# Nine orders and owners in a streaming encoder layer: norms, weight split, attention scaling, zeros

## The chip, the cores and the metric

The kernel runs on one core of one Trainium2 chip. TensorE (PE) multiplies matrices, VectorE (DVE) and ScalarE (ACT) work on vectors, GpSimd (POOL) helps, and SyncE (SP) issues most DMAs. The metric is the device time of one execution in microseconds; less is better. Three runs of the kernel before gave 1050.23, 1053.16 and 1054.89 us.

## The reference

One layer of an encoder on 544 tokens: 512 of a new stream (four tiles of 128) and 32 of a running stream (the tile called SAMPLE, number 4). All weights are float32.

```
h   = RMSNorm(x);  c = h @ w_in                       # 1824 + 1536 + 2048 columns
A   = RWKV-7 time mixing of c: token shift, LoRA decay/rate/gate,
      per-token matrix state S (8 heads, 64x64), head layer norm, + bonus, * gate
Bd  = differential attention, 4 heads; RMSNorm over each head's 128 outputs
      * subln * (1 - lam_init)
mix = sigmoid(gA) * (A @ w_out_a) + sigmoid(gB) * (Bd @ w_out_b)
x   = x + RMSNorm(mix @ w_o)
x   = x + RMSNorm(SwiGLU(RMSNorm(x)))                 # D_FF = 2816
```

Besides the two outputs the layer gives new keys, values, the state S and the last shifted row of each stream.

## The kernel before

Every large product is made in three passes of a rounded format: a weight w is split into w_hi (rounded) and w_lo = w - w_hi, an activation likewise, and PE adds hi*hi, hi*lo and lo*hi into one accumulator (`three`). Channels lie on partitions, tokens on columns, 272 of them to a bank. A block of 128 output channels over all 544 tokens is one "dense" step, and two accumulators of two banks (dps) take turns. Four further banks (side) serve everything else in turn: each step of the list takes the next bank, and PE may write it only after the reader four fills earlier has drained it.

Weights come in units of 128 x 1024 (512 KB). SP loads unit u into one of two raw buffers once POOL has split unit u-2 (`w_split`); POOL splits it (L718 w_hi, L723 w_lo) into one of two slots once PE has finished the last block that uses the slot (`seg_done`). POOL starts unit after unit at the dense steps of its own queue, so its other work (the start of the block inverse, "xi"; the affine part of the group norm, "yrs", L787 to L798; the diagonal blocks, L782) stands between them.

One list, `schedule()`, gives the order of all steps, and each engine walks through it and issues its own part, so every engine has a fixed queue. The parts of the list that matter here:

- The first norm. normA squares a tile on ACT and scales it on DVE (L1638); normB transposes it on PE (L1055), ACT copies h_hi, DVE subtracts h_lo (L1607). The first two blocks of c are done in token halves: tiles 0 and 1 first, then tiles 2, 3 and 4. SP issues the loads of x, the constants (cst) and some twenty-five small parameters before unit 2's weight load.
- Attention. attS, attC, attP and attO are one head of one tile. After all heads of the prompt, "oscale" makes the reciprocals, "oA" scales a tile's heads by its reciprocal and by subln (DVE, L1699), "ofin" transposes it on PE and splits it into o_hi (ACT) and o_lo (DVE). Pieces of the gate projections (gB, gA) are woven in as filler for PE.
- The state stage, from about 280 to 555 us. For each tile a 128 x 128 triangular inverse is built in levels: wm (PE product, DVE mask L1821), wd (PE product, DVE subtraction L1829, then an expansion L1614 or L1834 with a transpose L1837), wt (PE transpose, ACT copy). Two groups g of four heads go side by side. Beside the inverse of tile t+1 run the chain of states of tile t (chain0, q, ya, yb, chain1, L928 to L963) and the group norm of tile t-1: ymean, yvar, yrs, then yfin (the gate's product on PE L1184, L1185, gating on DVE L1869) and ysplit (y_hi on ACT L1443, y_lo on DVE L1875, which releases the bank).
- "init0" zeroes three buffers on DVE (L1760 to L1762) and then lets ACT load the running stream's state into one of them (L1378).
- The output projections. outB needs o; outE does blocks 0 to 5 for tiles 0 and 1, outL and outA the rest once the last group norm is split. DVE multiplies by the gate and adds outB's part, ACT and DVE split the result into S (L1993 to L2011, L1522, L1525). Units of outE are split on POOL at the steps of outE.
- "zw" and "zS" gather the sums of squares of the later norms (L1895, L1913), make the root on ACT (L1474) and the reciprocal on DVE (L1916).

## Time and profile before

| | us |
|---|---|
| median of three runs | 1053.16 |
| the profiled execution | 1049.86 |
| its span | 1048.1 |
| PE busy | 995.7 |
| DVE busy | 463.5 |
| ACT busy | 277.5 |
| POOL busy | 552.8 |

In a timeline row the first number is the start in microseconds from the span's start, the second how long the row's instructions took together, then engine, line, instruction, output and inputs, and how many there were. In square brackets stands how long the engine was idle before, and which engine's instruction released it. "SPq" and "ACTq" are DMA issues in an engine's queue. In a row of the chain of waits there are start, length, engine and line. A row of the windows gives busy time and count for PE, PEld (weight load), DVE, ACT and POOL, then the granted clock of PE as a share of full speed, the DMA share and GB/s. Full speed is 2.4 GHz, and the other level is 1.2 GHz.

### The profile page before, as it was taken

How to read it: one execution, taken by the hardware profiler on the slowest of the kernel's cores; microseconds unless marked ns; L12 is line 12 of the kernel's file. 1: busy time of each engine (PE TensorE's matmuls, PEld its weight loads, DVE VectorE, ACT ScalarE, POOL GpSimd, SP SyncE). 2: the span in 40 equal slices, each digit the busy share in tenths (PEclk: the TensorE clock that was granted, in tenths of full speed). 3: DMA queues.
4: the chain of work that ended last, by engine and by line, in shares of the span. 5: the costliest groups of instructions: out<-in, count | busy, mean ns of one | idle time of the engine just before them, and what ended most of it. 6: DMA issues, size and time to landing. Idle time of an engine off the chain costs nothing.

```text
span 1048.1 us, 22126 instructions
## 1 busy us (share of the span) xinstructions
PE 995.7 (95%) x8886; PEld 942.4 (90%) x8886; DVE 463.5 (44%) x895; ACT 277.5 (26%) x788; POOL 552.8 (53%) x605
## 2 busy tenths in 40 slices
PE   5899999999999999989988998999999999999996
PEld 4899999988878887878888998999999999999996
DVE  4456478277666455555445354333333333200003
ACT  4223354245533123322211353100110100011101
POOL 4677899633444134241446812565565565656571
PEclk9999999999999999999999999999999999999999
DMA  8232322432223100132014612322322323232332
GB/s 267 62 82 81 81 70 72 124 113 72 66 73 83 38 32 33 33 119 106 26 54 133 184 45 61 98 82 80 100 80 83 97 80 90 83 93 76 93 91 86
DMA packets 138111, 89.70 MB, mean 86 GB/s; under 512 B 5258, under 2 KB 130032, under 8 KB 138032
## 3 DMA queue, kind: packets, MB, share of 16 engines
q1 hardware_dynamic: 129508, 73.17, 24.4%
q10 hardware_dynamic: 8524, 15.42, 4.2%
q8 instruction: 56, 0.92, 0.4%
q14 instruction: 23, 0.19, 0.1%
HBM read 79.39 MB, written 9.19 MB: 85 GB/s over the span
## 4 chain that ended last, share of the span: by engine, by line
PE 83%; DVE 8%; POOL 3%; ACT 2%; issue 2%; DMA 1%; ACTq 0%; DVEq 0%; SPq 0%; POOLq 0%
PE dense L981 67%; PE side L1055 3%; PE side L1098 1%; POOL w_lo L723 1%; PE side L933 1%; PE side L1124 1%; DVE gt L1793 1%; PE side L907 1%; PE side L897 1%; PE side L1175 1%; DMA xs<-in_x_prompt 1%; PE side L963 1%; PE side L847 1%; PE side L928 1%; DVE z L1937 1%
## 5 line engine op out<-in xcount | busy, mean ns | idle before, releaser
L718 POOL TENSOR_SCALAR w_hi<-w_raw 128x256 fp32r<-128x256 f32 (+1 forms) x256 | 158.4, 637 | 369.7 <-PE dense L981 360.0
L723 POOL TENSOR_TENSOR w_lo<-w_raw,w_hi 128x256 fp32r<-128x256 f32 (+1 forms) x256 | 321.4, 1277 | 9.8
L981 PE MATMUL dense<-h_hi,w_hi 128*128 128x272 f32 (+2 forms) x1392 | 303.6, 296 | 10.4 <-DVE h_lo L1607 6.9
L981 PE MATMUL dense<-h_hi,w_lo 128*128 128x272 f32 (+2 forms) x1392 | 295.0, 290 | 0.0
L981 PE MATMUL dense<-h_lo,w_hi 128*128 128x272 f32 (+2 forms) x1392 | 294.2, 289 | 0.0
L981 PEld LDWEIGHTS dense<-h_hi,w_hi 128*128 128x128 f32 x1392 | 221.7, 190 | 21.3 <-issue 8.6
L981 PEld LDWEIGHTS dense<-h_lo,w_hi 128*128 128x128 f32 x1392 | 222.4, 190 | 0.0
L981 PEld LDWEIGHTS dense<-h_hi,w_lo 128*128 128x128 f32 x1392 | 221.4, 190 | 0.0
L981 PE MATMUL dense<-S,w_hi 128*128 128x272 f32 (+2 forms) x648 | 109.2, 289 | 0.0
L981 PEld LDWEIGHTS dense<-S,w_hi 128*128 128x128 f32 x648 | 92.2, 188 | 0.1
L981 PE MATMUL dense<-S,w_lo 128*128 128x272 f32 (+2 forms) x324 | 68.2, 288 | 0.0
L1971 DVE SCALAR_TENSOR_TENSOR S<-z,S 128x544 f32 (+1 forms) x22 | 53.5, 2430 | 22.5 <-ACT S L1502 22.5
L1965 DVE TENSOR_TENSOR z<-z,dense 128x544 f32<-128x544 f32 (+2 forms) x23 | 15.9, 696 | 97.1 <-PE dense L981 97.1
L1904 DVE TENSOR_TENSOR z<-side,gain 128x512 f32<-128x512 f32 x7 | 4.8, 691 | 114.6 <-ACT h_hi L1465 114.6
L981 PEld LDWEIGHTS dense<-S,w_lo 128*128 128x128 f32 x324 | 51.1, 188 | 0.0
L1502 ACT ACTIVATE S<-z 128x544 f32 (+1 forms) x22 | 14.5, 661 | 132.3 <-DVE z L1965 132.3
L981 PE MATMUL dense<-S 128*128 128x288 f32 (+1 forms) x336 | 45.3, 291 | 0.0
L981 PEld LDWEIGHTS dense<-S 128*128 128x128 f32 x336 | 42.8, 188 | 0.4 <-DVE S L2011 0.2
L1960 DVE SCALAR_TENSOR_TENSOR z<-z,dense 128x544 f32<-128x544 f32 (+2 forms) x23 | 15.9, 696 | 59.2 <-ACT z L1495 55.3
L1495 ACT ACTIVATE z<-dense 128x544 f32<-128x544 f32 x21 | 13.1, 625 | 97.4 <-PE dense L981 97.4
L792 POOL TENSOR_TENSOR AR<-AR 128x256 f32<-128x256 f32 (+1 forms) x10 | 6.5, 650 | 52.7 <-DVE AR L1860 52.7
L1291 ACT ACTIVATE early<-side,amax 128x128 f32<-128x128 f32 (+4 forms) x40 | 19.9, 499 | 35.7 <-DVE amax L1673 35.6
(270 smaller groups left out, 1393.3 us busy)
## 6 DMA issues: line engine op xcount, KB each, us to landing
w_raw<-in_w_ffn_in SPq DMA_DIRECT2D x44, 512.0 KB, 3.8
w_raw<-in_w_in SPq DMA_DIRECT2D x43, 512.0 KB, 3.9
w_raw<-in_w_ffn_out SPq DMA_DIRECT2D x16, 448.0 KB, 3.6
gates<-gst ACTq DMA_DIRECT2D x16, 272.0 KB, 2.0
w_raw<-in_w_o SPq DMA_DIRECT2D x8, 512.0 KB, 3.8
w_raw<-in_w_ffn_out SPq DMA_DIRECT2D x8, 512.0 KB, 3.7
w_raw<-in_w_out_a SPq DMA_DIRECT2D x5, 512.0 KB, 3.5
mb<-gates ACTq DMA_DIRECT2D x1, 2176.0 KB, 8.7
```

Of the source, the lines that this page charges most:

```text
L718: ins = nc.gpsimd.tensor_scalar(hi[:, q], w_raw[:, slot, q], 1.0, 0.0, ALU.mult, ALU.add)
L723: ins = nc.gpsimd.tensor_tensor(lo[:, q], w_raw[:, slot, q], hi[:, q].bitcast(F32), ALU.subtract)
L847: ins = pe.matmul(b[32 * q:32 * q + 32, 0:64], xt[:, g, q, :], mce[:, g, q, :], start=True, stop=True)
L897: ins = pe.matmul(b[0:n, h * 64:(h + 1) * 64], gt[0:n, g, h, 0:n], tok[0:n, g, 2, h, :], start=True, stop=True)
L981: ins = pe.matmul(acc[:, bk, 0:tn], w, r[:, t0:t0 + tn], start=first and n == 0, stop=final and n == 2)
L1055: ins = pe.transpose(b[0:m, c0:c0 + n], src, ident[0:n, 0:n])
L1291: drain(f_act(probs[0:n, pb, m, 0:keys], b[0:n, 0:keys], ACT.Exp, bias=amax[0:n, 2 * pb + m:2 * pb + m + 1], scale=SCALE, accum_out=asum[0 ...
L1495: f_act(f_t.rearrange("p (a b) -> p a b", a=2), pa[:, :, 0:HALF], ACT.Tanh, scale=0.5).then_inc(s_["f_tanh"], 1)
L1502: f_act(dst, f_s.unsqueeze(1), ACT.Copy, scale=0.5).then_inc(s_["f_hi"], 1)
L1960: ins = vec.scalar_tensor_tensor(out=fs, in0=ft, scalar=1.0, in1=ga_, op0=ALU.add, op1=ALU.mult)
L1965: ins = vec.tensor_tensor(fs, fs, gb_, ALU.mult)
L1971: vec.scalar_tensor_tensor(out=lo, in0=f_s.unsqueeze(1), scalar=0.5, in1=hi.bitcast(F32), op0=ALU.mult, op1=ALU.subtract).then_inc(s_["f_l ...
```

## The change

Nine edits, none of which changes what is computed:

1. The norm of tiles 2 and 3 moves ahead: the third tile is transposed before the first dense group, the fourth before the second.
2. Unit 0 gets split buffers of its own (w0_hi, w0_lo), and unit 2's split has no wait on PE. On SP the small parameters are issued after unit 2's load, the constants before it.
3. oA moves from DVE to ACT, scaling by the reciprocal alone. subln is loaded as one value per partition and applied in ofin, behind the transpose, by ACT and DVE.
4. The three memsets move from DVE to POOL, which waits for the last ofin; ACT's load of the state moves behind the next three steps (init1); DVE waits for the zeros at its first "e".
5. In wd, DVE subtracts for both groups first and expands both afterwards.
6. yfin and ysplit of a tile are issued one tile later, after "e" and a filler, and in the order g0, g0, g1, g1.
7. POOL splits the second outE unit at the second half of outB 7, and the third at outE 1.
8. outA's mixing is done in two halves of 272 tokens.
9. The sums of squares are reduced in zw, before the product, no longer in zS.

```diff
@@ -104,6 +104,7 @@
 OUT_LATE = [("outL", 2), ("outL", 3), ("outL", 4), ("outL", 5), ("outA", 6), ("outA", 7), ("outL", 0), ("outL", 1)]
+MIX_PIECE = {d: sum(1 + (e[0] == "outA") for e in OUT_LATE[:n]) for n, d in enumerate(OUT_LATE)}
@@ -184,7 +185,7 @@
     rows = [[(st, t, g) for g in range(2)] for st in ("ymean", "yvar", "yrs")[:2 + (t >= SAMPLE - 1)]]
-    return rows + [[(st, t, g) for st in ("yfin", "ysplit") for g in range(2)]]
+    return rows + [[(st, t, g) for g in range(2) for st in ("yfin", "ysplit")]]
@@ -212,7 +213,7 @@
     norms = skew(NT, "normA", "normB")
-    s = norms[:5] + first_pair[:1] + norms[5:7] + first_pair[1:2] + norms[7:] + first_pair[2:] + [("params",)]
+    s = norms[:7] + first_pair[:1] + norms[7:9] + first_pair[1:2] + norms[9:] + first_pair[2:] + [("params",)]
@@ -276,17 +277,18 @@
         s += [("ofin", t)] + filler(t < SAMPLE)
-    s += weave([[("init0",)]] + first[-3:], [filler(1) for _ in range(3)])
+    s += weave([[("init0",)]] + first[-3:], [filler(1) for _ in range(3)]) + [("init1",)]
+    yfin = []
...
-        s += filler(t == SAMPLE) + both("wu", t) + filler(t == SAMPLE) + both("e", t) + filler(1)
+        s += filler(t == SAMPLE) + both("wu", t) + filler(t == SAMPLE) + both("e", t) + filler(1) + yfin
...
-                s += weave(invert_rows(t + 1), [c00, ymean, f0, c01, yvar, f1, q, [], f2, ya, f3, yfin, c10, f4, c11])
+                s += weave(invert_rows(t + 1), [c00, ymean, f0, c01, yvar, f1, q, [], f2, ya, f3, [], c10, f4, c11])
@@ -441,6 +443,9 @@
     ga = sb("ga", [P, 8, TOK], at=phase2)
+    w0_hi = sb("w0_hi", [P, D], F32R, at=region)
+    w0_lo = sb("w0_lo", [P, D], F32R, at=region)
+    region.close()
@@ -488,7 +493,7 @@
     orst = sb("orst", [P, NT * BH], at=phase2)
-    subln = sb("subln", [P, BV], at=phase2)
+    subln = sb("subln", [P, 1], at=phase2)
@@ -580,6 +585,15 @@
+
+    def mix_halves(d):
...
+        i, acc = d[1], dps[BLOCK[d] % 2]
+        if d[0] == "outA":
+            cuts = [(bk * HALF, HALF, acc[:, bk, 0:HALF]) for bk in range(2)]
+        else:
+            cuts = [(2 * P, TOK - 2 * P, acc[:, 0, 0:TOK - 2 * P])]
+        return [(S[:, i, 0, a:a + n], S[:, i, 1, a:a + n], ga[:, i, a:a + n], mb[:, i, a:a + n], c) for a, n, c in cuts]
@@ -643,7 +657,6 @@
         def load_parameters():
-            sp.dma_start(cst[:, :], i_["cst"][:, :]).then_inc(s_["cst_loaded"], 16)
@@ -659,7 +672,7 @@
                 sp.dma_start(lamv[:, n, :], i_[name][0].partition_broadcast(P)).then_inc(s_["att_loaded"], 16)
-            sp.dma_start(subln[:, :], i_["diff_subln"][0].partition_broadcast(P)).then_inc(s_["att_loaded"], 16)
+            sp.dma_start(subln[:, :], i_["diff_subln"][0].rearrange("(p o) -> p o", o=1)).then_inc(s_["att_loaded"], 16)
@@ -673,6 +686,8 @@
                 x_load(SAMPLE)
+                sp.dma_start(cst[:, :], i_["cst"][:, :]).then_inc(s_["cst_loaded"], 16)
+            elif u == 3:
@@ -735,10 +750,10 @@
             else:
-                hi, lo = w_hi[:, u % 2, :], w_lo[:, u % 2, :]
-                if u >= 2:
...
-                    v = next(v for v in range(u - 2, -1, -2) if UNITS[v][0] != "woA" or UNITS[v][1] == 5)
+                hi, lo = (w_hi[:, u % 2, :], w_lo[:, u % 2, :]) if u else (w0_hi[:, :], w0_lo[:, :])
+                if u >= 3:
...
+                    v = next(v for v in range(u - 2, 0, -2) if UNITS[v][0] != "woA" or UNITS[v][1] == 5)
@@ -760,7 +775,9 @@
                 ahead = UNIT_OF[step[1:3]][-1][0] + 1
-                units_up_to(min(ahead, UNIT_OF[("outE", OUT_EARLY[-1])][0][0]) if step[1] == "outE" else ahead)
+                units_up_to(min(ahead + step[2] % 2, UNIT_OF[("outE", OUT_EARLY[-1])][0][0]) if step[1] == "outE" else ahead)
+            elif step == ("dense", "outB", 7, 1, 2):
+                units_up_to(UNIT_OF[("outE", 2)][0][0])
@@ -776,6 +793,13 @@
                                         ALU.add).then_inc(s_["xb_init"], 1)
+            elif k == "init0":
...
+                pool.wait_ge(s_["rw_done"], CT)
+                landed(pool, ("ofin", SAMPLE), "o")
+                G(nc.gpsimd.memset(sio[:, :, :], 0.0))
+                G(nc.gpsimd.memset(ebd[:, :, :, :, :], 0.0))
+                nc.gpsimd.memset(mbd[:, :, :, :, :], 0.0).then_inc(s_["zeroed"], 1)
@@ -1028,6 +1052,8 @@
                     hi, lo = w_hi[:, u % 2, c:c + P], w_lo[:, u % 2, c:c + P]
+                    if u == 0:
+                        hi, lo = w0_hi[:, c:c + P], w0_lo[:, c:c + P]
@@ -1314,8 +1340,19 @@
                 A.mark(f_act(orms[0:n, a:b_], ossq[0:n, a:b_], ACT.Sqrt, scale=1.0 / BV, bias=EPS), s_["o_rms"], "o_rms")
+            elif k == "oA":
+                t = step[1]
+                n = TILES[t][1]
+                act.wait_ge(s_["o_rst"], 1 + (t == SAMPLE))
+                for h in range(BH):
+                    o = otok[0:n, t, h * BV:(h + 1) * BV]
+                    ins = f_act(o, o, ACT.Copy, scale=orst[0:n, t * BH + h:t * BH + h + 1])
+                ins.then_inc(s_["o_scaled"], 1)
...
-                halves(o_hi, step, "o", *TILES[step[1]], "o_hi_done", 0)
+                t0, n = TILES[step[1]]
+                b = full_bank(act, step, "o")
+                f_act(o_hi[:, :, t0:t0 + n], b[:, 0:4 * n].rearrange("p (k n) -> p k n", k=4), ACT.Copy,
+                      scale=subln[:, :]).then_inc(s_["o_hi_done"], 1)
@@ -1371,7 +1408,7 @@
                 A.mark(f_act(t2, t2, ACT.Exp, scale=-1.0), s_["rw_e2"], "rw_e2")
-            elif k == "init0":
+            elif k == "init1":
@@ -1517,13 +1554,9 @@
                     turn = OUT_LATE.index(d)
-                    act.wait_ge(s_["mixed"], turn + 1)
-                    if kind == "outA":
-                        f_act(S[:, i, 0, :].rearrange("p (a b) -> p a b", a=2), dps[BLOCK[d] % 2][:, :, 0:HALF], ACT.Copy,
-                              scale=0.5).then_inc(s_["mix_hi"], 1)
-                    else:
-                        f_act(S[:, i, 0, 2 * P:TOK], dps[BLOCK[d] % 2][:, 0, 0:TOK - 2 * P], ACT.Copy, scale=0.5).then_inc(
-                            s_["mix_hi"], 1)
+                    for half, (hi, _, _, _, acc) in enumerate(mix_halves(d)):
+                        act.wait_ge(s_["mixed"], MIX_PIECE[d] + half + 1)
+                        f_act(hi, acc, ACT.Copy, scale=0.5).then_inc(s_["mix_hi"], 1)
@@ -1690,19 +1723,15 @@
                 dve.wait_ge(s_["o_rms"], step[1] + 1)
-                V(vec.reciprocal(orst[0:n, a:b_], orms[0:n, a:b_]))
-            elif k == "oA":
-                t = step[1]
-                n = TILES[t][1]
-                for h in range(BH):
-                    o = otok[0:n, t, h * BV:(h + 1) * BV]
-                    ins = vec.scalar_tensor_tensor(out=o, in0=o, scalar=orst[0:n, t * BH + h:t * BH + h + 1],
-                                                   in1=subln[0:n, :], op0=ALU.mult, op1=ALU.mult)
-                V.mark(ins, s_["o_scaled"], "o_scaled")
+                V.mark(vec.reciprocal(orst[0:n, a:b_], orms[0:n, a:b_]), s_["o_rst"], "o_rst")
...
-                low(o_hi, o_lo, step, "o", t0, n, "o_hi_done", t + 1, 0)
+                b = full_bank(dve, step, "o")
+                dve.wait_ge(s_["o_hi_done"], t + 1)
+                drain(vec.scalar_tensor_tensor(out=o_lo[:, :, t0:t0 + n], in0=b[:, 0:4 * n].rearrange("p (k n) -> p k n", k=4),
+                                               scalar=subln[:, :], in1=o_hi[:, :, t0:t0 + n].bitcast(F32), op0=ALU.mult,
+                                               op1=ALU.subtract), step, "o")
@@ -1755,11 +1784,6 @@
                 V.mark(vec.tensor_tensor(kx, kx, t2, ALU.mult), s_["rw_done"], "rw_done")
-            elif k == "init0":
...
-                V(vec.memset(sio[:, :, :], 0.0))
-                V(vec.memset(ebd[:, :, :, :], 0.0))
-                V.mark(vec.memset(mbd[:, :, :, :, :], 0.0), s_["zeroed"], "zeroed")
@@ -1793,6 +1817,8 @@
                 elif st == "e":
+                    if (t, g) == (0, 0):
+                        dve.wait_ge(s_["zeroed"], 1)
@@ -1827,17 +1853,20 @@
                 drain(vec.tensor_tensor(xv, xv, b[0:n, 0:64].rearrange("p (b s) -> p b s", s=s), ALU.subtract), step, "d")
-                landed(dve, step, "d")
-                if lv + 1 < len(LEVELS):
-                    expand(lv + 1, t, g)
-                elif nblocks(t) > 1:
-                    V.mark(vec.tensor_tensor(xe32[:, g, :, :], xp[:, g, :].unsqueeze(1).broadcast_to([P, 2, P]),
-                                             cst[:, K_BB:K_BB + 4:2].unsqueeze(2).broadcast_to([P, 2, P]), ALU.mult),
-                           s_["xe_set"], "xe_set")
-                    V.mark(vec.transpose(xb[:, g, :], xp[:, g, :]), s_["xb_last"], "xb_last")
-                else:
-                    V.mark(vec.transpose(xt64[0:n, g, :, 0:n], xp[0:n, g, :].rearrange("p (h i) -> p h i", h=4)),
-                           s_["x64_set"], "x64_set")
+                if g == 0:
+                    continue
+                for gg in range(2):
+                    landed(dve, (k, lv, t, gg), "d")
+                    if lv + 1 < len(LEVELS):
+                        expand(lv + 1, t, gg)
+                    elif nblocks(t) > 1:
+                        V.mark(vec.tensor_tensor(xe32[:, gg, :, :], xp[:, gg, :].unsqueeze(1).broadcast_to([P, 2, P]),
+                                                 cst[:, K_BB:K_BB + 4:2].unsqueeze(2).broadcast_to([P, 2, P]), ALU.mult),
+                               s_["xe_set"], "xe_set")
+                        V.mark(vec.transpose(xb[:, gg, :], xp[:, gg, :]), s_["xb_last"], "xb_last")
+                    else:
+                        V.mark(vec.transpose(xt64[0:n, gg, :, 0:n], xp[0:n, gg, :].rearrange("p (h i) -> p h i", h=4)),
+                               s_["x64_set"], "x64_set")
@@ -1887,6 +1916,9 @@
                 dve.wait_ge(s_["z_sq"], (i + 8 * (part == "B") if i < 8 else 30 + (part == "B")) + 1)
+                if i >= 7:
+                    for n, a, b_ in Z_SUMS[(i - 7, part)][1]:
+                        V.mark(vec.tensor_reduce(ssq[0:n, a:b_], zsq[0:n, a:b_, :], AX.X, ALU.add), s_["z_sum"], "z_sum")
@@ -1909,8 +1941,6 @@
                 first_sum, pieces = Z_SUMS[step[1:]]
-                for n, a, b_ in pieces:
-                    V.mark(vec.tensor_reduce(ssq[0:n, a:b_], zsq[0:n, a:b_, :], AX.X, ALU.add), s_["z_sum"], "z_sum")
@@ -1996,20 +2026,17 @@
+                    block_full(dve, d)
+                    halves = mix_halves(d)
...
+                    for _, _, gate, other, a2 in halves:
+                        V(vec.scalar_tensor_tensor(out=a2, in0=gate, scalar=1.0, in1=a2, op0=ALU.add, op1=ALU.mult))
+                        V.mark(vec.tensor_tensor(a2, a2, other, ALU.add), s_["mixed"], "mixed")
+                    for half, (hi, lo, _, _, a2) in enumerate(halves):
+                        dve.wait_ge(s_["mix_hi"], MIX_PIECE[d] + half + 1)
+                        ins = vec.scalar_tensor_tensor(out=lo, in0=a2, scalar=0.5, in1=hi.bitcast(F32), op0=ALU.mult,
+                                                       op1=ALU.subtract)
+                    ins.then_inc(block_sem(d), 1)
```

## Rows read from the trace of the kernel before

**Rows 1.** The page's busy times by engine, whole span.

```profile
PE 995.7 (95%) x8886; PEld 942.4 (90%) x8886; DVE 463.5 (44%) x895; ACT 277.5 (26%) x788; POOL 552.8 (53%) x605
```

**Rows 2.** Timeline, 0 to 45 us: start, length, engine, instruction, idle before.

```profile
11.02 1.97 PE L1055 MATMUL side<-ident,xn 128*128 128x128 f32 x8 [0.95 <-DVE xn L1638]
...
12.65 2.73 DVE L1638 SCALAR_TENSOR_TENSOR xn<-xs,rstd,gain 128x1024 f32<-128x1024 f32 x1
...
16.76 0.58 PE L981 MATMUL dense<-h_hi,w_hi 128*128 128x256 f32 x1 [3.77 <-DVE h_lo L1607]
...
18.84 23.77 SPq L693 DMA_DIRECT2D w_raw<-in_w_in  x4
...
28.49 0.40 PE L981 MATMUL dense<-h_hi,w_hi 128*128 128x288 f32 x1 [1.52 <-DVE h_lo L1607]
...
32.12 1.51 POOL L718 TENSOR_SCALAR w_hi<-w_raw 128x256 fp32r<-128x256 f32 x4 [11.51 <-PE dense L981]
...
36.65 0.49 PE L981 MATMUL dense<-h_hi,w_hi 128*128 128x272 f32 x2 [1.43 <-POOL w_lo L723]
```

**Rows 3.** Timeline, 279 to 298 us, end of attention.

```profile
279.50 0.28 ACT L1311 ACTIVATE otok<-side 128x128 f32<-128x128 f32 x1
...
288.90 1.82 DVE L1699 SCALAR_TENSOR_TENSOR otok<-otok,orst,subln 128x128 f32<-128x128 f32 x3
...
292.17 1.13 DVE L1699 SCALAR_TENSOR_TENSOR otok<-otok,orst,subln 128x128 f32<-128x128 f32 x4
...
297.07 0.30 PE L1055 MATMUL side<-ident,xp 128*128 128x128 f32 x1 [1.31 <-ACT early L1291]
```

**Rows 4.** Timeline: POOL's first memset, and 324 to 332 us.

```profile
0.75 0.52 POOL L757 MEMSET g2b<- 96x512 f32 x1 [0.29 <-POOLq L2031]
...
324.26 0.91 DVE L1761 MEMSET ebd<- 128x1024 f32 x1 [0.28 <-DVE C L1760]
...
326.39 1.36 ACTq L1378 DMA_DIRECT2D C<-in_state_wkv  x2
...
328.17 0.63 PE L850 MATMUL side<-xte,tc 128*32 128x128 f32 x8 [1.64 <-ACT tc L1406]
...
331.56 0.46 POOL L775 TENSOR_TENSOR xb<-wa,cst 128x128 f32<-128x128 f32 x1 [6.70 <-DVE wa L1775]
```

**Rows 5.** Timeline of PE, 366 us.

```profile
366.69 0.33 PE L1055 MATMUL side<-ident,xp 128*128 128x128 f32 x1 [0.73 <-DVE xp L1829]
```

**Rows 6.** Timeline of PE: the three waits for the split's bank.

```profile
414.06 0.34 PE L928 MATMUL side<-wu,tok 64*64 64x64 f32 x4 [1.39 <-DVE y_lo L1875]
...
459.76 0.34 PE L928 MATMUL side<-wu,tok 64*64 64x64 f32 x4 [2.00 <-DVE y_lo L1875]
...
504.18 0.34 PE L928 MATMUL side<-wu,tok 64*64 64x64 f32 x4 [0.84 <-DVE y_lo L1875]
```

**Rows 7.** Timeline, 534 to 575 us, output projections.

```profile
534.01 0.72 DVE L1986 SCALAR_TENSOR_TENSOR mb<-mb,dense 128x544 f32<-128x544 f32 x1 [1.15 <-PE dense L981]
...
542.54 0.83 PE L1055 MATMUL side<-ident,mbd 128*128 128x128 f32 x4 [0.74 <-ACT AR L1397]
...
545.00 0.36 PE L981 MATMUL dense<-y_hi,w_hi 128*128 128x256 f32 x1 [1.64 <-POOL w_lo L723]
...
555.69 0.37 PE L981 MATMUL dense<-y_hi,w_hi 128*128 128x288 f32 x1 [2.15 <-DVE y_lo L1875]
...
574.12 0.40 PE L981 MATMUL dense<-y_hi,w_hi 128*128 128x288 f32 x1 [1.16 <-DVE S L2011]
```

**Rows 8.** A row of the windows, and two of the chain: start, length.

```profile
556.00:560.00 4.00, 4.00 (x22) 4.00 (x21) 1.39 (x3) 0.41 (x1) 0.00 (x0) 0.61 0.00 0
...
285.83 1.49 PE dense L981 x12
...
461.51 3.02 PE dense L981 x12
```

**Rows 9.** Timeline of DVE at the end.

```profile
1041.73 0.16 DVE L1913 TENSOR_REDUCE ssq<-zsq 128x2 f32<-128x16 f32 x1
```

15 lines of the change are left out of this document (1 added, 14 removed).

## The prediction, made before the changed kernel was built

> **What bounds the kernel now.** I read the busy times first, then every TensorE (PE) wait in order of time, then the other engines around each wait. PE is busy 995.7 of 1048.1 us [rows 1], so 52.4 us are all that orders and owners can win, apart from PE's own pace. No PE instruction is added or removed by the change. The waits fall into places that the nine edits name: the first norm [rows 2], the end of attention [rows 3], the first state tile [rows 4], the block inverse [rows 5], the group norm's split [rows 6], the output projections [rows 7], the sums of squares [rows 9]. A second loss is pace: four stretches run at half clock, 1.2 instead of 2.4 GHz, three behind waits of 1.31, 2.00 and 2.15 us and one behind two short ones at 365.6 and 366.7. One window shows a granted mean of 0.61, and twelve dense matmuls take 3.02 us instead of 1.49 [rows 8].
>
> **The change part by part.** The sum is made against the profiled execution: span 1048.1, its own time 1049.86.
>
> *Norm order at the start.* PE stands 3.77 us before its first dense group, which waits for h_lo of tile 1; the normalised tile 2 is ready at 12.65+2.73=15.38 [rows 2]. Its eight transposes go in front of that group. At the half clock eight take 1.97, so they end at about 17.4, 0.6 after the old start of 16.76. Against this, about 0.9 leaves the full-clock part, some 0.5 comes back because less dense work falls before the clock rises, 0.2 because tiles 3 and 4 are transposed apart, and the 1.52 wait at 28.49 shrinks to about 0.6, since only the 32 rows of tile 4 are left to copy and subtract. +0.6-0.9-0.5-0.2-0.9 = -1.9. Bounds: -3.4 (both waits half gone and the 0.9) and 0.
>
> *Unit 0 in its own buffer, parameters behind unit 2's load.* Unit 2 is split only after PE has left unit 0 (POOL idle 11.51 until 32.12), and PE waits 1.43 for it at 36.65 [rows 2]. Now POOL goes on from unit 1 at about 20.7 and has unit 2 by 27, so the 1.43 goes. On SP's queue, unit 2's load leaves at about 14.4 instead of 18.84; some twenty-five parameter DMAs, 9.9 us of issue, come behind it, so unit 3's load leaves at about 24.4, while POOL wants it at 32. The parameter transposes on PE come at about 33, after the last of these has left at 24.3. -1.4; bounds -1.43 and 0. What speaks against it: POOL now works beside VectorE's (DVE's) norm of tile 4, and a norm beside a split took 2.73 [rows 2]; it would end at 23 and is wanted at 25, so this is hidden, by 2 us.
> The Trainium skill (SBUF — State Buffer, Who interferes with whom) says that DVE with two SBUF inputs and GpSimd lock each other out of one port pair, and that ScalarE never waits there. The trace agrees: the scaling took about 0.6 a piece beside a split and 0.28 without one [rows 3]. By that rule the scaling is worth up to its upper bound below, 1.31, and the sum of the waits would be 11.6 and not 10.75; the same rule speaks against the early split of unit 2.
>
> *Attention scaling on ScalarE (ACT).* Twenty DVE operations become twenty ACT copies of 0.28 [rows 3]: 1.1 us a tile. The pieces of tiles 0 and 1 stand before the masks and subtractions that lead to the wait of 1.31 at 297.07, but a dense group between them hides the first; 0.5 reaches PE. For tile 4 ACT must wait for a reciprocal that stands behind inverse work on DVE, and three copies of the transposed output queue behind it by about 3 us; PE has dense groups there and their banks come free in time: nothing. -0.5; bounds -1.31 and +1.1 (one tile's copies uncovered).
>
> *Zeros on POOL.* Three memsets on DVE (0.91 for 1024 columns) and 1.36 of DMA issue on ACT stand before the copy tc; PE waits 1.64 for it [rows 4]. POOL has 6.70 us idle up to 331.56; its own memset of 512 columns took 0.52, so 512+1024+1024 cost about 2.6, and it waits for the end of attention, which is over by then. The 1.64 goes. The two issues now stand before the token copies of tile 0: of 1.36 I let 0.5 reach PE through the banks. -1.1; bounds -1.64 and -0.3.
>
> *Both groups' subtractions before the expansions.* The second transpose waited 0.73 because the first group's expansion and DVE transpose stood before its subtraction [rows 5]: -0.7. In twenty such places the first group's expansion comes one subtraction (0.2) later. At the next steps a dense group of 1.5 covers that; uncovered it is +4.4.
>
> *Split a tile later, group by group.* PE waits 1.39, 2.00 and 0.84 for a bank that y_lo releases [rows 6], as gating stands behind the inverse's last level on DVE. At the new place, after e and a dense group, DVE has less before it, but each group is now a serial chain DVE, ACT, DVE of about 1.3, and the next chain0 reuses the bank: I take 0.35 there, and 0.25 where the removed matmuls covered the subtraction, twice, and 0.1 for the third tile. -4.23+1.3 = -2.9; bounds -4.2 and 0.
>
> *Early weight split.* The second outE unit is split behind the group norm's POOL work; PE waits 1.64 for it at 545.00 [rows 7]. It will be split from the end of outB 7 on, shortly before 534.01 [rows 7], in front of that work, which then starts 0.9 later and so frees the second bank of the final transposes later: that takes 1.5 of the 1.64 and of a wait of 0.74 before it [rows 7]. -0.9; bounds -2.4 and +1. *Group order at outL:* the first six matmuls need group 0 alone, ready 1.3 earlier, the next six group 1 as before: of 2.15 [rows 7] 0.65 goes; bounds -2.15 and 0. *Halved mixing:* of 1.16 [rows 7] 0.2, as six short DVE operations replace three; bounds -1.16 and +0.3. *Sums first:* a reduction of 0.16 [rows 9] and the square root pass the product, 0.25 on two chains, one of them the tail: -0.5; bounds -0.8 and 0.
>
> Sum of the waits: 1.9+1.4+0.5+1.1+0.7+2.9+0.9+0.65+0.2+0.5 = 10.75.
>
> *Clock.* Each half-clock stretch costs about 1.5 (3.02-1.49) [rows 8], four 6.0. Waits of 1.64 [rows 4, 7] are not followed by one, so idle time alone doesn't decide; I take half: -3.0, bounds -6 and +3 (two new ones).
> The Trainium skill (TensorE: Matmul & The Clock Gate, Part 1) says that the throttled state is the default and activity releases it. By that rule all four could go, which is the third rival.
>
> 10.75+3.0 = 13.75: the profiled 1049.86 becomes 1036.1. That execution lies 3.3 below the median of the runs shown (1053.16), so for a median I forecast 1053.16-13.75 = 1039.4, say **1040**, with a range of its own of 1034 to 1047.
>
> **Rivals.**
> *Slower: DVE's queue is the bound of the state stage.* Place: from 300 to 555 us. The late expansions cost 4.4 and five tiles' split pairs hold DVE for 2x1.3 each, 13, all seen by PE. The other terms (10.75 without 0.7 and 2.9) give back 7.15, with no clock gain: +10.3, 1063. For it: most PE waits there name DVE. Against: the three waits in [rows 6] sum to 4.23 in 90 us, and dense groups stand between the steps. It decides once more than about 1.2 of each 1.3 hold is uncovered.
> *The waits change place.* The bank wait after the split, the token copies and the late POOL work fill what was freed; only head, zeros and sums stay: 1.9+1.4+1.1+0.5 = 4.9, 1048. For it: each freed wait has a next one within 0.5 us in my reckoning.
> *The clock stays up.* 10.75+6.0: 1036. For it: each drop follows a wait that an edit names.
> *The change doesn't do what it says:* the new buffer and the order at SP bring unit 2 no earlier, as its load shares the DMA engines with the constants; then 1.4 less, 1041.5, inside the forecast.
>
> **How the numbers follow.** Forecast 0.60 (with the last rival), clock stays up 0.16, waits change place 0.17, slower 0.07. A measurement of this kernel tells 0.5%, 5.3 us, from no change. Faster: 0.60+0.16 and half of 0.17, 0.84; same 0.10, slower 0.06. The range of 8 in 10 is 1033 to 1049.
>
> **What would show it.** Right: the first dense matmul at about 17.4 behind three tiles' transposes, no POOL wait at 33; no wait at the copy tc; L928 without y_lo waits over 0.5; DVE without otok; POOL's outE unit before its AR work; fewer windows with a clock under 1. Wrong: PE's first wait behind yfin's transposes over 1 us; POOL's AR work so late that the final transposes wait over 2 us; the token copies holding sk by 1.3; as many half-clock stretches as before, elsewhere. If PE's idle time falls by less than 6 us the sum is wrong whatever the time says.

## The result, and the profile after

The kernel after took 1039.07 us in the median (1037.57 to 1040.89, four runs) against 1053.54 (1050.23 to 1054.89, four runs): ratio 0.9868, 95% interval 0.984 to 0.9896. Run again later in six runs it gave 1040.21 (1037.25 to 1041.94), ratio 0.9881 [0.9856, 0.9907] against eleven runs of before at 1052.05. The forecast was 1040. Its profiled execution took 1040.89 (span 1039.1), 1.8 above its median, while that of before lay 3.7 below its own; so the two traces differ by 9.0 us and the medians by 14.5.

The page's busy times after [rows 1]:

```profile
PE 993.6 (96%) x8886; PEld 939.6 (90%) x8886; DVE 451.2 (43%) x878; ACT 284.0 (27%) x810; POOL 557.1 (54%) x608
```

PE's idle time (span less busy) fell from 52.4 to 45.5, by 6.9 where the forecast had 10.75. PE's timeline after, at the places of [rows 2 to 7]:

```profile
15.45 1.97 PE L1081 MATMUL side<-ident,xn 128*128 128x128 f32 x8 [2.45 <-DVE xn L1671]
17.07 0.56 PE L1005 MATMUL dense<-h_hi,w_hi 128*128 128x256 f32 x1
...
26.64 0.40 PE L1005 MATMUL dense<-h_hi,w_hi 128*128 128x288 f32 x1 [0.76 <-DVE h_lo L1640]
...
292.99 0.30 PE L1081 MATMUL side<-ident,xp 128*128 128x128 f32 x1 [0.41 <-ACT early L1317]
...
327.26 1.17 PE L911 MATMUL side<-AR,C 64*128 64x256 f32 x4 [0.42 <-ACT tok L1421]
...
425.74 0.34 PE L952 MATMUL side<-wu,tok 64*64 64x64 f32 x4 [0.43 <-DVE y_lo L1904]
...
470.63 0.34 PE L952 MATMUL side<-wu,tok 64*64 64x64 f32 x4 [0.41 <-DVE y_lo L1904]
...
533.12 0.41 PE L1081 MATMUL side<-ident,mbd 128*128 128x128 f32 x2 [2.03 <-DVE y_lo L1904]
538.09 0.73 PE L1201 MATMUL side<-AR,cst 128*128 128x64 f32 x4 [1.26 <-ACT AR L1467]
544.36 0.37 PE L1005 MATMUL dense<-y_hi,w_hi 128*128 128x288 f32 x1 [0.93 <-DVE y_lo L1904]
545.85 0.58 PE L1005 MATMUL dense<-y_hi,w_hi 128*128 128x288 f32 x1 [0.45 <-DVE y_lo L1904]
...
563.27 0.40 PE L1005 MATMUL dense<-y_hi,w_hi 128*128 128x288 f32 x1 [1.18 <-DVE S L2037]
```

The waits of the head, of the first state tile and of the inverse are gone or small. Two of 2.03 and 1.26 at 533 and 538 are new, and so is one of 1.25 at 499.69, which the section on the experiments shows. Summed over the rows of its timeline, PE's waits went from 43.9 to 36.9 us: from 15.8 to 12.3 up to 100 us, from 14.6 to 9.6 between 290 and 520, from 6.5 up to 8.3 between 520 and 600, and from 4.5 to 4.2 behind.

The clock: before, four stretches lay under full speed [rows 8]; after, one. PE's windows of 4 us after (the clock is the third number from the end):

```profile
544.00:548.00 4.00, 3.19 (x15) 3.02 (x16) 0.95 (x4) 0.23 (x1) 0.76 (x3) 0.73 0.00 0
548.00:552.00 4.00, 3.60 (x23) 3.37 (x21) 2.43 (x7) 0.82 (x2) 1.75 (x2) 0.84 0.00 0
```

Every run lists its mean granted clock. Eleven runs of before average 0.9915, six of after 0.9965. Over 1050 us that is some 9.0 and 3.6 us lost to the clock, 5.4 less. With 7.0 of waits it makes 12.4, an estimate that lies between the two measured differences of the medians, 14.5 and 11.8. It mixes the waits of one execution with the clock of many. Within the profiled pair the mean clocks are 0.992 and 0.996, about 4 us apart; with 7.0 that makes 11, and 9.0 were measured, since some 2 us came back inside PE's busy time.

### The profile page after: what moved, and what is told of

It reads as the page before. It is cut to its first block, busy times and chain, and to the rows that moved or that the text cites. A ratio compares the mean times of both kernels' runs of the same rounds, so it can differ in the third digit from the quotient of the medians.

```text
span 1039.1 us, 22129 instructions
## 1 busy us (share of the span) xinstructions
PE 993.6 (96%) x8886; PEld 939.6 (90%) x8886; DVE 451.2 (43%) x878; ACT 284.0 (27%) x810; POOL 557.1 (54%) x608
## 4 chain that ended last, share of the span: by engine, by line
PE 82%; DVE 6%; POOL 4%; DMA 3%; ACT 3%; issue 1%; ACTq 0%; DVEq 0%; SPq 0%; POOLq 0%
PE dense L1005 66%; PE side L1081 3%; DMA w_raw<-in_w_o 2%; POOL w_lo L738 1%; PE side L1124 1%; PE side L1150 1%; PE side L957 1%; POOL S L738 1%; PE side L931 1%; PE side L921 1%; PE side L1201 1%; DMA xs<-in_x_prompt 1%; PE side L911 1%; PE side L871 1%; PE side L987 1%
## 5 line engine op out<-in xcount | busy, mean ns | idle before, releaser
L1005 PE MATMUL dense<-h_hi,w_hi 128*128 128x272 f32 (+2 forms) x1392 | 302.7, 295 | 4.4 <-DVE h_lo L1640 2.5
L1005 PE MATMUL dense<-h_hi,w_lo 128*128 128x272 f32 (+2 forms) x1392 | 293.8, 289 | 0.0
L1005 PE MATMUL dense<-h_lo,w_hi 128*128 128x272 f32 (+2 forms) x1392 | 293.1, 288 | 0.0
L1005 PEld LDWEIGHTS dense<-h_hi,w_hi 128*128 128x128 f32 x1392 | 220.9, 189 | 15.0 <-issue 7.0
L1005 PEld LDWEIGHTS dense<-h_lo,w_hi 128*128 128x128 f32 x1392 | 221.4, 189 | 0.0
L1005 PEld LDWEIGHTS dense<-h_hi,w_lo 128*128 128x128 f32 x1392 | 220.2, 189 | 0.0
L1005 PE MATMUL dense<-S,w_hi 128*128 128x272 f32 (+2 forms) x648 | 109.2, 289 | 0.1
L1005 PEld LDWEIGHTS dense<-S,w_hi 128*128 128x128 f32 x648 | 92.2, 188 | 0.5 <-issue 0.4
L1005 PE MATMUL dense<-S,w_lo 128*128 128x272 f32 (+2 forms) x324 | 68.2, 288 | 0.0
L1005 PEld LDWEIGHTS dense<-S,w_lo 128*128 128x128 f32 x324 | 51.1, 188 | 0.0
L1539 ACT ACTIVATE S<-z 128x544 f32 (+1 forms) x22 | 14.5, 659 | 132.3 <-DVE z L1995 132.3
L1005 PE MATMUL dense<-S 128*128 128x288 f32 (+1 forms) x336 | 45.3, 291 | 1.7 <-POOL S L738 1.7
L1005 PEld LDWEIGHTS dense<-S 128*128 128x128 f32 x336 | 42.8, 188 | 2.5 <-issue 2.2
```

Of the source, the lines that this page charges most:

```text
L1005: ins = pe.matmul(acc[:, bk, 0:tn], w, r[:, t0:t0 + tn], start=first and n == 0, stop=final and n == 2)
L1539: f_act(dst, f_s.unsqueeze(1), ACT.Copy, scale=0.5).then_inc(s_["f_hi"], 1)
```

## The experiments

Each of the first eight undoes one part of the change in the kernel after. They ran once each, beside single runs of before at 1053.80 and 1054.77. The profiled spans of the kernel after itself were 1039.1 and 1036.4 in two executions, so an end time under 3 us apart says nothing here, and I read them by the wait at its place and by the distance between two marks with the same work between them. Three marks serve: the wait for the first weight split at about 104 (L1005 w_lo), the waits for `gain` that begin the inverse of each tile (308.94, 350.22, 392.82 and 437.92 after), and the last wait for S at 563.27.

### The norm's order

```diff
-    s = norms[:7] + first_pair[:1] + norms[7:9] + first_pair[1:2] + norms[9:] + first_pair[2:] + [("params",)]
+    s = norms[:5] + first_pair[:1] + norms[5:7] + first_pair[1:2] + norms[7:] + first_pair[2:] + [("params",)]
```

> The changed kernel with edit 1 undone (norm steps in the old order). The waits-add-up theory: the group of tiles 2 to 4 of the first block starts at about 28.5 instead of 26.64, with a wait near 1.5 in front of it, and every later mark up to 540 us lies 1.8 later; span about 1041. The theory that waits change place: the 1.8 is there at 30 us but less than 0.5 of it at 540.

1044.14, span 1042.4. The mark at 104.49 came at 108.49, 4.0 later. The waits up to there grew from 12.3 to 14.25, and the next two windows hold a half-clock stretch that neither before nor after has; PE's wait and the windows of this kernel:

```profile
29.12 0.41 PE L1005 MATMUL dense<-h_hi,w_hi 128*128 128x288 f32 x1 [1.52 <-DVE h_lo L1640]
```

```profile
28.00:32.00 4.00, 2.88 (x13) 2.88 (x14) 1.07 (x4) 0.08 (x1) 0.00 (x0) 0.67 0.86 228
32.00:36.00 4.00, 4.00 (x29) 4.00 (x29) 0.00 (x0) 0.75 (x3) 0.00 (x0) 0.90 0.17 47
```

Without that stretch (about 1.5) the order is worth about 2.5, against a forecast of 1.9, and it isn't given back: the four `gain` marks, too, lie 3.9 to 4.0 later. The same wait of 1.52 was followed by no stretch before [rows 2].

### Unit 0's buffer and the parameters' place

```diff
-                hi, lo = (w_hi[:, u % 2, :], w_lo[:, u % 2, :]) if u else (w0_hi[:, :], w0_lo[:, :])
-                if u >= 3:
+                hi, lo = w_hi[:, u % 2, :], w_lo[:, u % 2, :]
+                if u >= 2:
...
-            elif u == 3:
+            elif u == 2:
                 load_parameters()
```

> Edit 2 undone alone (unit 0 in slot 0, parameters issued before unit 2's load). Waits add up: PE waits about 1.4 for w_lo at about 34.8, and later marks up to 540 us lie 1.4 later; span about 1040.5. Waits change place: the POOL wait of 0.96 at 104.5 shrinks by as much, and nothing is left at 200 us.

1040.99, span 1039.2. The wait is back, whole, but the mark at 104 is only 0.6 later than after's, where 1.4 was forecast (in the eleven traces with this part and the norm's new order it stood at 103.62 to 104.94, so it is 0.2 to 1.5 later than there). The wait for POOL behind that mark is 0.96 as before, so the 1.45 was not given back there:

```profile
34.07 0.49 PE L1004 MATMUL dense<-h_hi,w_hi 128*128 128x272 f32 x2 [1.45 <-POOL w_lo L737]
```

### The attention's scaling back on VectorE, subln left behind the transpose

```diff
-                act.wait_ge(s_["o_rst"], 1 + (t == SAMPLE))
...
-                    ins = f_act(o, o, ACT.Copy, scale=orst[0:n, t * BH + h:t * BH + h + 1])
+                    ins = vec.tensor_scalar(o, o, orst[0:n, t * BH + h:t * BH + h + 1], None, ALU.mult)
```

> The scaling of attention's output by the reciprocal goes back from ACT to DVE (as a multiplication by one value per partition; subln stays in ofin). Prediction's step: the wait of 0.41 at 293.0 becomes 0.9 to 1.3, later marks lie 0.5 to 0.9 later, and perhaps a half-clock stretch comes back behind it (1.5 more). Rival, ACT's own queue was the cost of the move: marks at 310 us lie earlier than in the changed kernel, as tile 4's scaling no longer holds ACT.

1035.23, span 1033.4, the shortest of all. DVE's scaling and PE's wait in this kernel, then ACT's scaling in the kernel after:

```profile
285.34 2.37 DVE L1724 TENSOR_SCALAR otok<-otok,orst 128x128 f32<-128x128 f32 x4
...
288.42 0.86 DVE L1724 TENSOR_SCALAR otok<-otok,orst 128x128 f32<-128x128 f32 x4
...
292.64 1.79 DVE L1724 TENSOR_SCALAR otok<-otok,orst 128x128 f32<-128x128 f32 x8
...
292.81 0.30 PE L1081 MATMUL side<-ident,xp 128*128 128x128 f32 x1 [0.62 <-ACT early L1317]
```

```profile
293.27 1.27 ACT L1349 ACTIVATE otok<-otok,orst 128x128 f32<-128x128 f32 x4
...
295.31 1.26 ACT L1349 ACTIVATE otok<-otok,orst 128x128 f32<-128x128 f32 x4
```

The wait is 0.2 longer on DVE, but from it to the first `gain` mark this kernel takes 15.16 and every one of the twelve other traces of this study 15.94 to 15.97, since ACT's copies stand in front of the inverse's copies there: the new owner costs 0.6. The eight operations in front of the wait take 3.23 here (2.37 + 0.86) and took 3.69 before (four from 288.90 on in 2.56, of which [rows 3] shows three, and four in 1.13), so dropping subln saves DVE under 0.5 us there. The wait is 0.7 shorter than before's 1.31 with DVE as owner in both kernels. The rest of the way to after's end (1039.1, and 1036.4 in its second trace) is not the owner: there is no half-clock stretch in this trace and no wait for weights at 580 to 592, places that the edit doesn't touch.
The Trainium skill (SBUF — State Buffer, Who interferes with whom) has DVE and GpSimd lock each other out of a shared port pair.
The trace agrees, for the form without subln too: POOL split from 285.52 to 288.32, and the four operations at 285.34 took 0.59 each, while those at 288.42 and 292.64, where POOL stood idle, took 0.22.

### Zeros back on VectorE

```diff
-                G(nc.gpsimd.memset(ebd[:, :, :, :, :], 0.0))
-                nc.gpsimd.memset(mbd[:, :, :, :, :], 0.0).then_inc(s_["zeroed"], 1)
+                V(vec.memset(ebd[:, :, :, :], 0.0))
+                V.mark(vec.memset(mbd[:, :, :, :, :], 0.0), s_["zeroed"], "zeroed")
```

> Edit 4 undone: memsets on DVE, the load of the state before the next three steps. Waits add up: the 1.64 in front of the last inverse product comes back, the 0.42 before sk goes and sk's products take 2.45 instead of 3.00, so marks at 337 lie 1.1 later (0.7 to 1.6). If the two DMA issues had cost PE nothing in the new place, 1.6 later.

1041.98, span 1040.2. From the first to the second `gain` mark 43.20, after 41.28: the part is worth 1.9, over the bound of 1.64. PE's wait of this kernel, and POOL's memsets of the kernel after:

```profile
323.01 0.63 PE L867 MATMUL side<-xte,tc 128*32 128x128 f32 x8 [2.04 <-ACT tc L1436]
```

```profile
320.09 0.52 POOL L800 MEMSET C<- 128x512 f32 x1
320.67 0.95 POOL L801 MEMSET ebd<- 128x1024 f32 x1
321.68 0.95 POOL L802 MEMSET mbd<- 128x1024 f32 x1
```

A memset costs nearly the same on both engines (0.91 on DVE in [rows 4]), and POOL still waited 2.47 us for its next work at 325.10. The two DMA issues held the token copies for 0.42 (at 327.26 above), near the 0.5 forecast; this kernel has no such wait, and its products there take 2.45 where those of after take 3.00. But it waits 0.90 for rb at 334.30, as before did at 339.47. So 2.04 + 0.90 go and 0.42 + 0.55 come, 1.97 in all, close to the 1.9 measured.

### One group's subtraction and expansion at a time

```diff
-                if g == 0:
-                    continue
-                for gg in range(2):
-                    landed(dve, (k, lv, t, gg), "d")
...
+                landed(dve, step, "d")
+                if lv + 1 < len(LEVELS):
+                    expand(lv + 1, t, g)
```

> Edit 5 undone: each group's subtraction and expansion together. Prediction's step: a wait of about 0.7 before the second transpose of the last level in each of the tiles 1 to 3 (at 360, 402 and 448 us), so 2.2 later at 460, and perhaps a half-clock stretch again. The slower rival (late expansions cost 0.2 in each of twenty places): marks at 460 lie up to 4 earlier than in the changed kernel, or the 0.7s are paid for by as much elsewhere.

1042.80, span 1041.0. PE's waits of this kernel:

```profile
361.37 0.33 PE L1081 MATMUL side<-ident,xp 128*128 128x128 f32 x1 [0.73 <-DVE xp L1855]
...
406.21 0.33 PE L1081 MATMUL side<-ident,xp 128*128 128x128 f32 x1 [0.83 <-DVE xp L1855]
...
451.68 0.33 PE L1081 MATMUL side<-ident,xp 128*128 128x128 f32 x1 [0.73 <-DVE xp L1855]
```

One wait [rows 5] was in the trace of before; three come back. For the other two tiles the trace of before shows what covered them: not another wait, but work. Sixteen products of yfin (L1184, L1185) stood between the inverse's product and the second transpose, which then waited for nothing; the bank wait of 1.39 [rows 6] comes behind it.

```profile
410.03 0.43 PE L847 MATMUL side<-gain,xt 128*32 128x64 f32 x16
410.39 0.49 PE L1184 MATMUL side<-C,g2a 128*128 128x128 f32 x2
...
412.06 0.39 PE L1185 MATMUL side<-C,g2b 128*128 128x128 f32 x2
412.28 0.38 PE L1055 MATMUL side<-ident,xp 128*128 128x128 f32 x2
```

Edit 6 takes these products away from there, and so makes two of the three waits that edit 5 removes. The stretch from 350.22 to 461.47 takes 3.5 longer, 1.4 of it a half-clock stretch at 360 to 368, so about 2.1 without the clock. That is what was expected of this run (2.2), and three times the 0.7 of the prediction, which had the old place in view.

### The split's old place, and its old order too

```diff
-        s += ... both("e", t) + filler(1) + yfin
-                s += weave(invert_rows(t + 1), [c00, ymean, f0, c01, yvar, f1, q, [], f2, ya, f3, [], c10, f4, c11])
+        s += ... both("e", t) + filler(1)
+                s += weave(invert_rows(t + 1), [c00, ymean, f0, c01, yvar, f1, q, [], f2, ya, f3, yfin, c10, f4, c11])
```

That is the first kernel, with the new order of groups; the second has the old order as well:

```diff
-    return rows + [[(st, t, g) for g in range(2) for st in ("yfin", "ysplit")]]
+    return rows + [[(st, t, g) for st in ("yfin", "ysplit") for g in range(2)]]
```

> Only the place of edit 6 undone; the order g0, g0, g1, g1 stays. If the place is what counts, as I think: waits for y_lo as in the old place with the old order, 1.4, 2.0 and 0.8 at L952, since gating stands behind the inverse on DVE; the two waits at outL stay 0.93 and 0.45. If the order is what counts, the waits at L952 stay under 0.6.

> Edit 6 undone whole: old place and old order of the group norm's split. Waits add up: L952 (the chain's first product) waits 1.4, 2.0 and 0.8 for y_lo at about 405, 450 and 492 and no longer 0.43 and 0.41, so the mark of outE 0 lies 2.9 to 3.4 later, 4.5 if a half-clock stretch follows one of them; the wait at outL is 2.1 in one piece and not 0.93 and 0.45. DVE's-queue rival: less than 1 later.

1038.08 (span 1036.3) and 1042.69 (span 1040.5). With the old place the bank waits are back, with 1.20, 1.06 and 0.43; the first two of that kernel:

```profile
404.29 0.34 PE L952 MATMUL side<-wu,tok 64*64 64x64 f32 x4 [1.20 <-DVE y_lo L1904]
...
449.23 0.34 PE L952 MATMUL side<-wu,tok 64*64 64x64 f32 x4 [1.06 <-DVE y_lo L1904]
```

And yet the place gains nothing in these executions: from the third `gain` mark to the last wait for S, PE waits 11.8 after, 10.6 with the old place and 10.8 with place and order undone. The stretch itself takes 170.45, 167.36 and 170.34, of which half-clock stretches cost 1.7, 0 and 5.1 by the granted clock. At the bank the new place wins 1.85 (2.69 less 0.43 + 0.41), and more than that is lost at 499.69 and 538.09, 1.25 + 1.26. ACT writes each final state into one small buffer and stores it by a DMA, and the second group's copy waits until the first one's store has landed. ACT's rows, of the kernel after and of the old place:

```profile
495.54 0.39 ACTq L1247 DMA_DIRECT2D out_wkv_prompt<-dtmp  x1
499.06 0.27 ACT L1458 ACTIVATE dtmp<-side 64x128 f32<-64x128 f32 x1 [3.56 <-DMA out_wkv_prompt<-dtmp]
...
536.74 0.27 ACT L1458 ACTIVATE dtmp<-side 64x128 f32<-64x128 f32 x1 [3.62 <-DMA out_wkv_sample<-dtmp]
```

```profile
497.59 0.38 ACTq L1247 DMA_DIRECT2D out_wkv_prompt<-dtmp  x1
499.33 0.27 ACT L1458 ACTIVATE dtmp<-side 64x128 f32<-64x128 f32 x1 [1.77 <-DMA out_wkv_prompt<-dtmp]
```

In before, too, it landed in 1.77. The obvious suspect for the doubling, the next weight load, is ruled out. SP issues it at 497.99 after and at 500.04 with the old place, 2.45 behind the first store in both, and 2.43 to 2.46 behind it in all fourteen traces, late or not. Its packets come later still: in the window from 498.50 to 499.00, the last before ACT goes on, the DMA engines move nothing (share and GB/s are the last two numbers).

```profile
498.50:499.00 0.50, 0.00 (x0) 0.00 (x0) 0.00 (x0) 0.00 (x0) 0.00 (x0) 1.00 0.00 0
499.00:499.50 0.50, 0.00 (x0) 0.00 (x0) 0.00 (x0) 0.41 (x2) 0.00 (x0) 1.00 0.41 84
```

What was under way besides the store is in the DMA queues of the window from 495.54 to 498.50 after (packets, MB, share), and of 497.59 to 500.50 with the old place:

```profile
q10 hardware_dynamic: 272, 0.07, 11.4%
q8 instruction: 1, 0.02, 3.1%
```

```profile
q10 hardware_dynamic: 272, 0.07, 10.7%
```

The 272 packets are the store. The other is one packet of 16 KB in the queue named "instruction"; it took 1.48 us from 496.32 on, and the store's last seventeen packets, some 4 KB, began only at 497.79. Of the twelve traces in which ACT waits for these stores, 24 stores in all, fifteen landed after 2.3 to 3.8 us, and each of them had such a packet in flight before its own last one; nine landed in 1.76 to 1.78, and none of them had. So the lateness goes with where an instruction packet falls, which edit 6 doesn't set by itself: the kernel with edit 5 undone has the new place and both stores in time. No run changes that packet alone, so this cause is read from the traces and not tested.

The spread that it leaves is wide: the kernels with the norm's order or unit 0 undone differ from after only in the first 40 us, and PE waits 10.2 in this stretch in both. With two store buffers and the new place (below) it waits 9.2, 1.4 less than with the old place. In each of these three the clock costs 3.4 here, and a slower PE waits less, so the numbers flatter the new place.

The group order alone does its work: with it undone the wait at outL is 2.14, after 0.93 + 0.45, 0.76 less (forecast 0.65).

### The weight split in its old place

```diff
-                units_up_to(min(ahead + step[2] % 2, UNIT_OF[("outE", OUT_EARLY[-1])][0][0]) if step[1] == "outE" else ahead)
-            elif step == ("dense", "outB", 7, 1, 2):
-                units_up_to(UNIT_OF[("outE", 2)][0][0])
+                units_up_to(min(ahead, UNIT_OF[("outE", OUT_EARLY[-1])][0][0]) if step[1] == "outE" else ahead)
```

> Edit 7 undone: outE's later units split at outE's own steps. Prediction's step: the wait of 2.03 before the second final transpose shrinks to about 1.2, a wait of 1.6 for w_lo comes back before outE 2, the mark of outL lies 0.4 to 0.9 later. Rival, the early split gained nothing because it delays the group norm on POOL by as much: outL's mark within 0.3.

1037.90, span 1036.1. PE's two waits of this kernel, then POOL's work in the kernel after:

```profile
531.18 0.41 PE L1079 MATMUL side<-ident,mbd 128*128 128x128 f32 x2 [0.97 <-DVE y_lo L1902]
...
533.21 0.36 PE L1003 MATMUL dense<-y_hi,w_hi 128*128 128x256 f32 x1 [1.62 <-POOL w_lo L738]
```

```profile
523.15 1.05 POOL L733 TENSOR_SCALAR w_hi<-w_raw 128x1024 fp32r<-128x1024 f32 x1 [11.49 <-PE dense L1005]
524.29 2.37 POOL L738 TENSOR_TENSOR w_lo<-w_raw,w_hi 128x1024 fp32r<-128x1024 f32 x1
526.62 0.73 POOL L816 TENSOR_TENSOR AR<-AR 128x256 f32<-128x256 f32 x1
```

0.97 + 1.62 = 2.59 undone; 2.03 + 1.26 = 3.29 after, of which the 1.26 is the store again. The w_lo wait of 1.62 goes, as forecast, but the group norm's POOL work starts at 526.62 instead of 524.67, 1.95 later where I had 0.9, and the final transposes wait 1.06 longer for it; the store takes the rest. Counted from the fourth `gain` mark, outL's first wait comes 1.4 earlier with edit 7 undone (542.72 after 437.69, against 544.36 after 437.92), which neither expectation allowed; 1.26 + 0.66 of longer store waits make up all of it (here the first store wait is 0.59, the second absent). Without the stores the edit gains 0.56; as it ran, it was worth nothing, against -0.9.

### Versions that go on from there

> The changed kernel again, beside the three variants on the same chip. Its ratio to the kernel before lies within 0.985 to 0.989; spans near 1039, one half-clock stretch near 548 us, and PE waits of about 0.4 and 1.3 for POOL's w_o units near 579 and 592.

This is the kernel after once more, five rounds; the three that follow ran beside it on the same chip.

```diff
-            sout = dtmp[:, 0:2 * 64].rearrange("p (k v) -> p k v", k=2)
+            sout2 = [dtmp[:, a:a + 2 * 64].rearrange("p (k v) -> p k v", k=2) for a in (0, 2 * 64)]
...
+                sout = sout2[g]
+                if g == 0:
                     act.wait_ge(stored, 16 * n_stored[0])
```

> The changed kernel, with the final states stored from two buffers, so that ACT need not wait for the first store before it copies the second. The waits of 1.25 at 499.7 and 1.26 at 538.1 go, so outL's mark lies 2.5 earlier. Waits add up: the end too, span 1036.6. Given back at woA (POOL and the w_o loads set the pace there): the waits for POOL near 579 and 592 grow from 1.7 to about 3, and the end moves by less than 1.2.

1039.44 (1036.80 to 1039.58, five runs), ratio 0.9862 [0.9835, 0.9889]. With a buffer for each group's store ACT goes on at once, and both PE waits of 1.2 are gone:

```profile
495.42 0.39 ACTq L1247 DMA_DIRECT2D out_wkv_prompt<-dtmp  x1
495.86 0.27 ACT L1460 ACTIVATE dtmp<-side 64x128 f32<-64x128 f32 x1 [0.46 <-PE side L1081]
```

From the fourth `gain` mark to the last wait for S the waits sum to 6.98, after 9.55 and 9.83 in its two traces, and that stretch takes 123.55 instead of 125.35 and 125.28. So it is shown that the new waits came from the one buffer. The time follows less far: this trace has two half-clock stretches between 532 and 546, outL's first wait comes 1.6 earlier and not 2.5, and the median moves by 0.8, within the scatter.

The second loads of x elsewhere (tile 4 at woA 3, tiles 0 and 1 in woB):

```diff
-                    elif kind == "woA" and i in (2, 4, 6):
-                        x1_load({2: 4, 4: 0, 6: 1}[i])
+                    elif d == ("woA", 3):
+                        x1_load(4)
+                    elif kind == "woB" and i in (0, 2):
+                        x1_load(i // 2, "x1_early")
```

> The changed kernel, with x loaded again for tiles 0 and 1 during woB instead of woA, tile 4 at woA 3. Theory that the second loads of x delay w_o's loads on the same DMA engines: POOL's waits for w_o fall from 5.5 to about 3, PE's waits of 0.39 and 1.29 go, the end comes 1.5 to 2.5 earlier. Rival, POOL's own 3.45 per unit is the pace: its waits fall little, and the end moves under 0.5.

1039.48 (1037.67 to 1040.73), ratio 0.9875 [0.9848, 0.9902]. It was to free the DMA engines for the weights that PE waits for at woA in the kernel after:

```profile
575.86 1.05 POOL L733 TENSOR_SCALAR S<-w_raw 128x1024 fp32r<-128x1024 f32 x1 [2.27 <-DMA w_raw<-in_w_o]
```

```profile
591.99 0.78 PE L1005 MATMUL dense<-S 128*128 128x288 f32 x4 [1.29 <-POOL S L738]
```

The wait is not in its trace, but neither is it in the second trace of the kernel after, where POOL waited 0.93 at the same unit. Of the thirteen traces with most of the change in, ten have it, the longest of each 1.1 to 1.9 us, and from the last wait for S to the first wait for h_lo behind woA they take 49.6 to 51.5 against 47.3 to 47.5. One of the ten is the last kernel below, which has x's loads moved too and still waits 1.36 at 576.70. So the loads of x do not decide; what does stays open.

Both together, and tile 4's final transposes one dense group later:

```diff
-            s += [("final", t, g) for g in range(2)] + filler(t < SAMPLE)
+            s += filler(t == SAMPLE) + [("final", t, g) for g in range(2)] + filler(t < SAMPLE)
```

> Both variants together, and the running stream's final transposes one dense group later, so that the 2.03 in front of them is covered. Waits add up: 2.5+2.0+1.7, 6.2 earlier than the changed kernel, span 1033. Given back at woA: under 3.5 earlier.

1036.77 (1036.08 to 1037.83), ratio 0.985 [0.9824, 0.9876]: the best of all in a median, 3.4 under the kernel after in the same rounds, whose fastest of six runs, 1037.25, is the only one within its range. The later transposes wait 0.58 instead of 2.03, but outL then waits 2.35 where it had 0.93 + 0.45; so that move gains next to nothing. Of the two expectations, 6.2 earlier and under 3.5, the second came true.

## Why the prediction was right

The time and the main mechanism were right: most of the named waits went, and nothing became a new bound. But it is luck that the total is so near: the waits gave 7.0 and not 10.75, the clock about 5.4 by the mean of all runs and not 3.0, and for the profiled execution itself, where the sum gave 1036.1, 1040.89 was measured.

- **Head** (norm order -1.9, unit 0 -1.4). The sum was right, its parts less so: undone by themselves they give about 2.5 and 0.6. The first dense matmul stood at 17.07 (forecast 17.4), no POOL wait followed, and the mark behind came 3.2 earlier (107.70 to 104.49), forecast 3.3. The wait at 28.49 became 0.76, not 0.6.
- **Attention scaling** (-0.5). The sign of the sum was right: 1.31 became 0.41. The reason was half wrong: with subln gone and DVE as owner the wait is 0.62, so ACT as owner gave 0.2 of it and took 0.8 back behind it, 0.6 in all. I had priced ACT's copies at 0.28 from a copy out of a bank; they took 0.32 each in a row.
- **Zeros** (-1.1, measured -1.9). Too small: the term lacks the 0.90 that PE waited for rb behind the old memsets, and the wait that came back was 2.04 and not 1.64. What the DMA issues cost in their new place, 0.42 + 0.55, was more than my 0.5.
- **Subtractions first** (-0.7, measured about -2.1). I counted the one wait that the trace of before showed. In the other two tiles the products of yfin covered it, and edit 6 moved them.
- **Split a tile later** (-2.9; measured +1.0 to +1.2 by the waits of this stretch, and -0.4 to -0.7 if the two kernels that differ from after at the start alone are taken for it). The term of the sum that failed is "-4.23+1.3 = -2.9". The price at the bank was right (0.43, 0.41, none), but there was less to win: with place and order undone the bank waits are 1.19, 1.06 and 0.84, 3.09 in all and not 4.23, and with the place alone undone 2.69. And in after, ACT waited 3.56 and 3.62 for two stores that land in 1.77 elsewhere, a term that no step of mine had.
- **Early weight split** (-0.9, measured about 0: -0.6 at its own two waits, +0.7 with the store). Of two ends I took the middle; the group norm's work came later by 1.95, not 0.9. The sign I had written for this, final transposes waiting over 2 us, stood at 2.03.
- **Group order at outL** -0.65, measured -0.76. **Halved mixing** -0.2, measured nothing: 1.16 [rows 7] and 1.18. **Sums first** -0.5: the part behind the last mark shrank from 7.84 to 7.42, and the one from 613 to 635 by 0.3; -0.7.
- **Not foreseen:** 1.7 at woA (0.39 + 1.29), when POOL waits 5.5 us for the loads of w_o in place of 2.6; in the second trace of the kernel after it is 2.5, and the 1.7 are not there. PE's busy time, too, fell by only 2.1, though three stretches of 1.5 went. The 2.4 did not come back as idle time, which outside the listed waits is 8.5 us before and 8.6 after, but as slower work: 0.7 at woA, 0.5 in the first state tile, about as much between 293 and 309, 0.3 in the head.
- **Clock** (-3.0). Half the stretches was my guess; three of four went in the profiled pair. By the granted clock each of them cost 1.7. How loosely it hangs on the waits the experiments show: no stretch with the scaling on DVE or the weight split in its old place, one in both traces of after, three with the split undone whole. My reading that each drop follows a wait doesn't hold either: with unit 0's part undone PE fell to half clock at 530.85, with no wait over 0.25 us since 500.45. The Trainium skill (TensorE: Matmul & The Clock Gate, Part 1) has the throttled state as the default that activity releases; the direction agrees, but which wait brings a stretch, no run here settles.

Of the rivals, "the waits change place" described edits 6 and 7 and not the sum; it forecast 1048. "The clock stays up" (1036) is what the two kernels without a stretch came near, 1035.23 and 1037.90 in one execution each. "DVE's queue is the bound" is refuted: the bank waits behind the split sum to 0.84 us. "No earlier unit 2" is refuted: after, no wait for POOL stands near 33 us, and undone the wait of 1.45 came back (by its own terms it forecast 1040 + 1.4 = 1041.4, not 1041.5).

What stays open: why the medians differ by 14.5 in one comparison and 11.8 in the other; the wait at woA; what brings a half-clock stretch; and, untested, whether the instruction packets alone make the stores late.

## What to carry to other kernels

Work can cover a wait of another chain: before moving work away, look at what stands behind it and would wait without it. Here the products of yfin had covered two waits of 0.7 to 0.8, so the edit beside it was worth three times its row. Price an edit against the kernel that the other edits leave, and not against the trace of before alone: without edit 6 the bank waits are 3.09 here and not the 4.23 of the trace of before. An engine that waits for a store to land before it reuses a small buffer takes on all of the store's scatter; a second buffer took both waits away. And check a suspect against the traces without the symptom: the weight load left 2.45 us behind the store in the good case as in the bad one. Undo a part by itself even where the whole was a success: here the place of the split and the early weight split brought nothing as they ran, and half of the scaling's move cost 0.6.
